# Two-network transformer kernel on one core: three RMS norms applied behind the products that use them

## The reference, cut to what matters

```python
def rms_norm(x, g):
    xf = x.astype(jnp.float32)
    y = xf * lax.rsqrt(jnp.mean(xf * xf, axis=-1, keepdims=True) + NORM_EPS)
    return (y * g.astype(jnp.float32)).astype(x.dtype)

def swiglu(h, w_gate, w_up, w_down):
    return (jax.nn.silu(h @ w_gate) * (h @ w_up)) @ w_down

def odd_mixer(h, positions, w_qkv, w_out):
    q, k, v = jnp.split((h @ w_qkv).reshape(b, s, 3 * DIL_HEADS, HEAD_DIM), 3, axis=2)
    o = dilated_attention(rope(q, positions), rope(k, positions), v)
    return o.reshape(b, s, -1) @ w_out

for layer in range(DEPTH):                      # DEPTH = 2
    x = x + mixers[layer](rms_norm(x, mix_norms[layer]))
    x = x + memory_cross_attention(rms_norm(x, xn), rms_norm(mem, mn), wq, wkv, wo)
    x = x + swiglu(rms_norm(x, fn), wg, wu, wd)
```

## Time and profile before

| | us |
|---|---|
| median of 3 runs | 2158.86 |
| lowest and highest run | 2158.0, 2161.35 |
| the profiled execution, its time | 2164.88 |
| its span in the trace | 2163.1 |
| PE busy | 2038.2 |
| DVE busy | 1088.8 |
| ACT busy | 864.9 |
| POOL busy | 166.6 |

### The profile page before, as it was taken

One profiled execution on the slowest core, in us unless ns is written; L12 is line 12 of the kernel. 1 busy time (PEld: TensorE's weight loads), 2 busy tenths in 40 slices (PEclk: granted clock), 3 DMA queues, 4 the chain that ended last, 5 costly groups with the idle time before them and its releaser, 6 DMA issues.

```text
span 2163.1 us, 34406 instructions
## 1 busy us (share of the span) xinstructions
PE 2038.2 (94%) x14816; PEld 1804.7 (83%) x14816; DVE 1088.8 (50%) x1683; ACT 864.9 (40%) x1227; POOL 166.6 (8%) x165
## 2 busy tenths in 40 slices
PE   7799899899998999999999999999999798999998
PEld 7769899889697999978688877777777687998997
DVE  5555544455555455523534445444444525566554
ACT  4554533343644444523622334222222425444442
POOL 0030100002204000001520000000000003000000
PEclk9899899999998999989999999999999999999999
DMA  7254387764744555512633334445444421664553
GB/s 215 90 187 156 106 199 201 189 173 156 234 156 118 181 189 166 157 55 65 189 108 102 103 98 137 158 154 170 142 149 145 131 74 29 187 192 143 176 178 107
DMA packets 327077, 317.09 MB, mean 147 GB/s; under 512 B 12917, under 2 KB 311676, under 8 KB 326670
## 3 DMA queue, kind: packets, MB, share of 16 engines
q1 hardware_dynamic: 320080, 297.82, 44.7%
q0 software_dynamic: 3904, 12.03, 2.8%
q10 hardware_dynamic: 2942, 5.04, 0.7%
HBM read 306.01 MB, written 8.85 MB: 146 GB/s over the span
## 4 chain that ended last, share of the span: by engine, by line
PE 77%; DVE 9%; DMA 7%; ACT 5%; issue 1%; POOL 0%; ACTq 0%; SPq 0%; DVEq 0%; POOLq 0%
PE acc L631 21%; PE acc L632 20%; PE acc L633 20%; DVE w_low L1713 5%; ACT w_high L1253 3%; DMA raw<-in_l_w_up 2%; PE pss L789 2%; PE pst L800 1%; PE acc L646 1%; PE acc L647 1%; PE acc L648 1%; DMA raw<-in_l_w_down 1%; DMA raw<-in_w_mod 1%; PE acc L718 1%; PE acc L815 1%
## 5 line engine op out<-in xcount | busy, mean ns | idle before, releaser
L1713 DVE TENSOR_TENSOR w_low<-raw,w_high 128x2048 fp32r<-128x2048 f32 (+3 forms) x252 | 539.4, 2140 | 398.2 <-ACT w_high L1253 397.6
L631 PE MATMUL acc<-normed,w_high 128*128 128x256 f32 (+2 forms) x2008 | 641.5, 319 | 21.3 <-DVE w_low L1713 20.2
L632 PE MATMUL acc<-normed,w_high 128*128 128x256 f32 (+2 forms) x2008 | 633.3, 315 | 0.0
L633 PE MATMUL acc<-normed,w_low 128*128 128x256 f32 (+2 forms) x2008 | 632.9, 315 | 0.0
L1253 ACT ACTIVATE w_high<-raw 128x2048 fp32r<-128x2048 f32 (+3 forms) x252 | 447.3, 1775 | 381.0 <-PE acc L633 296.2
L631 PEld LDWEIGHTS acc<-normed,w_high 128*128 128x128 f32 (+1 forms) x2008 | 386.9, 193 | 55.2 <-DVE w_low L1713 27.1
L633 PEld LDWEIGHTS acc<-normed,w_low 128*128 128x128 f32 (+1 forms) x2008 | 386.9, 193 | 22.8
L632 PEld LDWEIGHTS acc<-normed,w_high 128*128 128x128 f32 (+1 forms) x2008 | 387.1, 193 | 22.2
L631 PE MATMUL acc<-inner,w_high 128*128 128x256 f32 (+2 forms) x1232 | 388.4, 315 | 5.2 <-DVE inner L1726 2.4
L632 PE MATMUL acc<-inner,w_high 128*128 128x256 f32 (+2 forms) x1232 | 385.5, 313 | 0.0
L633 PE MATMUL acc<-inner,w_low 128*128 128x256 f32 (+2 forms) x1232 | 385.0, 312 | 0.0
(11 more groups left out here) (214 smaller groups left out, 2131.8 us busy)
## 6 DMA issues: line engine op xcount, KB each, us to landing
raw<-in_w_ff SPq DMA_DIRECT2D x64, 1024.0 KB, 5.5
raw<-in_w_mod SPq DMA_DIRECT2D x48, 1024.0 KB, 5.2
raw<-in_w_in SPq DMA_DIRECT2D x48, 512.0 KB, 3.8
raw<-in_l_w_gate SPq DMA_DIRECT2D x22, 1024.0 KB, 5.6
raw<-in_l_w_up SPq DMA_DIRECT2D x22, 1024.0 KB, 6.1
raw<-in_w_in SPq DMA_DIRECT2D x18, 1024.0 KB, 5.3
raw<-in_l_w_down SPq DMA_DIRECT2D x16, 1024.0 KB, 5.6
raw<-in_l_w_qkv SPq DMA_DIRECT2D x12, 1024.0 KB, 5.2
```

Of the source, the lines that this page charges most:

```text
L631: mm(dst, lh, rh, start=i == 0, stop=False)
L632: mm(dst, lh, rl, start=False, stop=False)
L633: ins = mm(dst, ll, rh, start=False, stop=i == n - 1)
L1713: V.tensor_tensor(WL[:, s % NSPLIT, 0:nw], RAW[:, slot_of[u], 0:nw], WH[:, s % NSPLIT, 0:nw].bitcast(F32), ALU.subtract).then_inc(w_low, 1)
```

## The change

In the three norms, x times the norm's weight (without the row of reciprocal roots) is split and multiplied; the row is applied to the products.

- `gained_highs` (ACT) writes the high part of x times weight straight from x as soon as a residual bank is added, and behind each pair the squares. `gained_low` (DVE) writes the low part. The buffer in between and `highs` are gone for these norms.
- PE begins the next product with tiles that arrive one by one (`one_by_one`), and does `mean_square` behind that first unit and `spread` behind the second.
- `rooted_row` (DVE) copies the spread row to SBUF (RROW, in `scores` 2). `times_row` (DVE) moves a product bank to SBUF and multiplies it with the row.
- FFN: the gate bank goes through `times_row`; ACT's silu reads and writes that SBUF tile; DVE multiplies it with the row again (for the up product) and then with the up bank. On ACT the copy of the next gate unit now stands ahead of silu.
- Mixer of layer 1: q and k go through `times_row` on DVE instead of ACT's copy. For v the row is needed along partitions: `spread(column=True)` makes it with four more matmuls (RCOL), and ACT's copies of v are scaled by it. The rotary products come one unit later behind their product. `memory(1)` moves behind the first `times_row`.

The diff (context cut, eight blanks of indentation left out):

```diff
@@ -179,7 +179,9 @@
 SCRATCH = VEC[:, 117:128]
-ROOTED, EPS2 = VEC[:, 244:252], VEC[:, 252:253]
+ROOTED, EPS2, RCOL = VEC[:, 244:252], VEC[:, 252:253], VEC[:, 253:255]
+RROW = SM[:, 2, 0:S]
+RROW2 = bass.AP(tensor=RROW.tensor, offset=RROW.offset, ap=[list(RROW.ap[0]), [0, 2], [1, S]])
 SKEW = nc.dram_tensor("skew", [2, 120, 64, 127], F32, kind="Internal").ap()
@@ -746,7 +749,7 @@
-    def spread(T, at=0, dst=PST, to=None):
+    def spread(T, at=0, dst=PST, to=None, column=False):
         w, sel = T // 4, const("spread")
@@ -754,6 +757,11 @@
                      start=True, stop=True)
+        if column:
+            for j in range(4):
+                lo = w * (j % 2)
+                ins = mm(dst[lo:lo + w, T + j // 2:T + j // 2 + 1], RSTD[:, at:at + w], sel[:, P * j:P * j + 1],
+                         start=True, stop=True)
         ins.then_inc(spread_done, 1)
@@ -885,6 +893,12 @@
+    def one_by_one():
+        base = st["store"]
+        st["store"] += KD
+        return lambda k: base + k + 1
     def turn_in(src):
@@ -909,10 +923,7 @@
     for l in range(2):
-        if l:
-            mean_square(sq1, KD, S)
-            spread(S)
-        ready = by_tile(S)
+        ready = one_by_one() if l else by_tile(S)
         st["store"] += 4
@@ -966,14 +977,20 @@
         else:
-            for i in range(9):
+            out = []
+            for i in range(10):
+                out.append(st["acc"])
                 if i < 8:
...
                     values(1)
-                if i:
-                    rotate(dil_raw[i - 1:i], const("rot64"), "dil", st["acc"] - 2 - (i > 1))
-            values(2)
+                if i == 0:
+                    mean_square(sq1, KD, S)
+                elif i == 1:
+                    spread(S, column=True)
+                else:
+                    rotate(dil_raw[i - 2:i - 1], const("rot64"), "dil", out[i - 2])
+            values(1)
             attention(dil_tasks, MODS, lead=lambda: values(1), tail=heads_product)
@@ -985,16 +1002,20 @@
         project(2, ot, m=4, kt=4, ready=by_head_tile(4))
-        mean_square(sq1, KD, S)
-        spread(S)
-        ready = by_tile(S)
+        ready = one_by_one()
         done = {}
...
             tiles = FFN_CHUNKS[c][1]
+            if kind == "in" and c == 0:
+                project(1, at_pair, ready=ready)
+                mean_square(sq1, KD, S)
+                project(1, at_pair)
+                spread(S)
+                project(tiles - 2, at_pair)
+            elif kind == "in":
+                project(tiles, at_pair)
             if kind == "in":
-                project(tiles, at_pair, ready=ready)
-                ready = None
                 st["store"] += tiles // 2
@@ -1290,6 +1311,24 @@
+    def gained_highs(units, gain):
+        nc.scalar.activation(SCRATCH[:, st["roots"] % 11:st["roots"] % 11 + 1], EPSC[:], ACT.Sqrt)
+        st["roots"] += 1
+        for u in range(units):
+            if u < units - 1:
+                split()
+            for i in range(4 * u // units, 4 * (u + 1) // units):
+                g = st["acc"] + i
+                act.wait_ge(acc_free[g % 4], g // 4 + 1)
+                for k in (2 * i, 2 * i + 1):
+                    st["store"] += 1
+                    nc.scalar.activation(at_pair.high[:, k, 0:S], XC[:, k, 0:S], ACT.Copy,
+                                         scale=VEC[:, gain + k:gain + k + 1]).then_inc(high_done, 1)
+                for k in (2 * i, 2 * i + 1):
+                    nc.scalar.activation(sq1[:, k, :], XC[:, k, 0:S], ACT.Square).then_inc(sq_done, 1)
+        st["acc"] += 4
     def root(nt, T, at=0, bias=EPSC):
@@ -1414,11 +1453,6 @@
     for l in range(2):
-        if l:
-            root(KD, S)
-            split()
-            highs(norm_chunks(S))
-            highs(mem_chunks())
         if l == 0:
@@ -1476,16 +1510,24 @@
         else:
-            act.wait_ge(skew_w, 16 * 18)
-            for i, dst in enumerate(dil_raw):
-                copy_out(dst, shape2, 64 ** -0.5 if i < 4 else 1.0)
+            g = st["acc"]
+            st["acc"] += 1
+            split()
+            root(KD, S)
+            split()
+            highs(mem_chunks())
+            split(7)
+            st["acc"] += 13
+            act.wait_ge(acc_free[g % 4], g // 4 + 1)
+            def v_lead(i):
+                b, free = bank()
+                for t in range(NB):
+                    ins = nc.scalar.activation(v_dil[:, t, S * i:S * i + S], b[:, S * t:S * t + S], ACT.Copy,
+                                               scale=RCOL[:, t:t + 1])
+                ins.then_inc(free, 1)
                 split()
-                st["acc"] += i > 0
-
-            def v_lead(i):
-                copy_out(v_dil[:, :, S * i:S * i + S], shape2)
-                split()
-                st["acc"] += i == 0
+                st["acc"] += i < 2
@@ -1515,27 +1557,30 @@
         attention(x_tasks, lead=lambda: vx_lead(1))
-        residual_squares(2, sq1, S)
-        root(KD, S)
+        gained_highs(2, vcol[f"l{l}_ffn_norm"])
         split()
-        highs(norm_chunks(S))
         for kind, c in ffn_turns:
...
                 for m in range(0, tiles, 2):
-                    b, free = bank()
-                    i, g = st["sig"], st["acc"]
-                    if m or c:
-                        act.wait_ge(stored, st["store"])
-                    nc.scalar.activation(SM[:, i % 2, :], b[:], ACT.Silu).then_inc(free, 1)
+                    i, g = st["sig"] % 2, st["acc"]
+                    st["acc"] += 1
+                    if m == c == 0:
+                        root(KD, S)
+                    split()
+                    act.wait_ge(acc_free[g % 4], g // 4 + 1)
+                    nc.scalar.activation(SM[:, i, :], SM[:, i, :], ACT.Silu).then_inc(gated, 1)
                     st["sig"] += 1
-                    split()
+                    g = st["acc"]
                     st["acc"] += 1
...
                 act.wait_ge(gain_done, 3)
-                residual_squares(4, sq1, S, gain=ROOTED if l else None)
+                if l:
+                    residual_squares(4, sq1, S, gain=ROOTED)
+                else:
+                    gained_highs(4, vcol["l1_mix_norm"])
             elif l and (kind, c) == ffn_turns[-2]:
@@ -1816,6 +1861,28 @@
+    def gained_low(m, gain):
+        for k in m:
+            st["store"] += 1
+            dve.wait_ge(high_done, st["store"])
+            V.scalar_tensor_tensor(at_pair.low[:, k, 0:S], XC[:, k, 0:S], VEC[:, gain + k:gain + k + 1],
+                                   at_pair.high[:, k, 0:S].bitcast(F32), ALU.mult, ALU.subtract)\
+                .then_inc(stored, 1)
+    def rooted_row(column=False):
+        spreaded()
+        if column:
+            link(V.tensor_copy(RCOL, PST[:, S:S + 2]))
+        link(V.tensor_copy(RROW, PST[:, 0:S]))
+    def times_row(dst, g, scale=1.0):
+        dve.wait_ge(acc_full, g + 1)
+        V.scalar_tensor_tensor(dst, PSACC[g % 4][:].rearrange("p (a n) -> p a n", a=2), scale, RROW2, ALU.mult,
+                               ALU.mult).then_inc(acc_free[g % 4], 1)
     def memory(l, lo=0, hi=4):
@@ -1996,11 +2063,8 @@
     for l in range(2):
-        norm(XC, norm_chunks(S), S, vcol[f"l{l}_mix_norm"], lead=None if l else split)
-        if l:
-            split()
-            memory(1)
         if l == 0:
+            norm(XC, norm_chunks(S), S, vcol["l0_mix_norm"], lead=split)
             split()
@@ -2028,14 +2092,24 @@
         else:
-            for i in range(9):
+            g = st["acc"]
+            st["acc"] += 1
+            split()
+            inverted(S)
+            split()
+            rooted_row(column=True)
+            dve.wait_ge(skew_w, 16 * 18)
+            times_row(dil_raw[0], g, 64 ** -0.5)
+            memory(1)
+            for i in range(1, 10):
+                if i < 8:
+                    times_row(dil_raw[i], st["acc"], 64 ** -0.5 if i < 4 else 1.0)
                 st["acc"] += 1
                 split()
-                if i:
-                    rope(dil_raw[i - 1:i], sin64)
-            split()
+                if i > 1:
+                    rope(dil_raw[i - 2:i - 1], sin64)
             attention(dil_tasks, MODS)
-            st["acc"] += 3
+            st["acc"] += 2
         for m in banks(8, S):
@@ -2045,12 +2119,14 @@
         st["acc"] += 3 + 2
-        for i in range(2):
-            for m in banks(8, S)[2 * i:2 * i + 2]:
-                residual_bank(m, None, S)
-            if i == 0:
+        gain = vcol[f"l{l}_ffn_norm"]
+        for m in banks(8, S):
+            residual_bank(m, None, S)
+            if m[0]:
+                gained_low([m[0] - 2, m[0] - 1], gain)
+            if m[0] == 2:
                 split()
-        norm(XC, norm_chunks(S), S, vcol[f"l{l}_ffn_norm"])
+        gained_low([KD - 2, KD - 1], gain)
         split()
@@ -2058,13 +2134,23 @@
                     st["acc"] += 1
-                    split()
```

(22 more changed lines are left out.)

1 line of the change is left out of this document (added).

## The result

The changed kernel takes 2168.13 us (median of 7 runs, 2165.6 to 2176.25), the kernel before beside it 2158.0 (7 runs, 2154.17 to 2161.35): 1.0057 times, 95% interval 1.0038 to 1.0077. The forecast was 2160.9, a plus of 2.0, with a range up to 2167.5. The four series of this kernel that there are by now give +12.3, +5.9, +7.7 and +4.6 us on the mean of their runs (standard errors 1.9, 1.5, 1.2, 1.5). Weighted by these that is +7.2.

What follows compares the result with a forecast made beforehand. TensorE, busy 94% of the span, was taken as the bound, so only its idle or slow stretches count. Terms -2.3 - 1.3 + 0.2 + 5.4 = +2.0 us on the median 2158.86 gave 2160.9, range 2158 to 2165 (8 in 10: 2152.5 to 2167.5).

Steps and rivals of the forecast that it cites:

- Layer 0's FFN norm: Layer 0's FFN: gate 0 without a gap, waits before up 0 and up 1; 2.3 us gained (1.0 to 3.1).
- it costs nothing, because up 2 waits for its DMA longer still: Layer 0's FFN: a low clock after the 2.5 us wait before up 1 costs 0, hidden by up 2's DMA wait.
- no term depends on what lies between: Whole kernel: the +2.0 us worked out on the profiled execution also holds for the median, 6.0 us lower.
- Layer 1's mixer norm: Layer 1's qkv units: 1.3 us gained (0 to 2.5) despite a 4.3 us wait before unit 3; v's half copies lose 0.2.
- the case for which the forecast had a gain of 0.6 only: Layer 1's mixer norm: the first 2.0 us of waiting also bring the clock down, leaving a gain of 0.6 us.
- Layer 1's FFN norm: Layer 1's FFN: GpSimd's bias addition holds VectorE's low parts to its end; 5.4 us lost (4.1 to 7).
- The second fall of the clock: Layer 1's FFN, behind the 2.5 us wait before up 1: low clock again, 1.5 us, half of it taken.
- The order that I called decided by 0.1 us: Layer 1's FFN norm: whether POOL's addition starts before gate 0's split; if so, 6.1 us lost instead of 4.8.
- The first rival: Layer 1's FFN norm: low parts not held by GpSimd, only the split; total -3.0, 2155.9 us, chance 0.15.
- nothing lands on the path: Steady FFN pairs: VectorE gets 1.4 us more a pair, yet the deciding step from up's end to the next split is unchanged.
- The slow rival: Layer 0's FFN pairs: silu waits behind a late gate's copy, up to 0.9 us a time, 4 to 5 us; 2165.5, chance 0.25.
- The sign that the prediction named for this rival: Layer 0's FFN: PE waits clearly longer than before for split weights, behind pairs whose gate landed late.

Runs made afterwards that it cites:

- the quiet pair: The kernel before and the changed kernel, each without 14 of GpSimd's 16 layout DMAs in layer 0's FFN: 2149.47 and 2152.44 us.
- mixer_only: Only layer 1's mixer norm changed, against the kernel before: 2153.62 us, ratio 0.9983.
- l0_ffn_only: Only layer 0's FFN norm changed, against the kernel before: 2158.04 us, ratio 0.9994.
- l1_ffn_only: Only layer 1's FFN norm changed, against the kernel before: 2163.82 us, ratio 1.002.
- whole_pieces: All three norms changed and GpSimd's bias addition cut into 16 instructions, against the kernel before: 2153.49 us, ratio 0.9994.
- l0_mixer_pieces: Layer 0's FFN norm and layer 1's mixer norm changed, bias addition in 16 pieces, against the kernel before: 2166.7 us, ratio 1.0012.
- mixer_pieces: Only layer 1's mixer norm changed, bias addition in 16 pieces, against the kernel before: 2153.36 us, ratio 0.9977.
- silu_first: All three norms changed, silu and VectorE's gate product ahead of the next gate's copy and split, against the kernel before: 2167.22 us, on another chip 2158.77.
- silu_pieces: All three norms changed, silu ahead of the next gate's copy, bias addition in 16 pieces, against the kernel before: 2162.88 us, then 2149.89.
- quiet_whole: All three norms changed, 14 of GpSimd's 16 layout DMAs in layer 0's FFN left out, against the kernel before: 2152.44 us, ratio 0.9982.

## Why the prediction was wrong

The forecast was +2.0; measured were +10.1 by the medians of the first series and +7.2 (1.4) over all four. Two terms were put at nothing that are not nothing: the place of silu in the steady pairs (4.1 us) and, in layer 0, the clock behind the new wait before up 1 (1.6 us).

- **Layer 0's FFN norm, forecast -2.3.** Gate 0 without a gap, 0.75 us of wait before up 0 (0.9 forecast), up 1 at +22.7 (+22.7) behind a wait of 2.35 (2.5): right. Wrong is "it costs nothing, because up 2 waits for its DMA longer still". The clock takes 1.6 us in the quiet pair. The wait that was to hide it, 1.96 us before up 2, stands in the trace of before and in none of the other 19. So it was wrong, too, that "no term depends on what lies between" the traced execution and the median. The norm is worth about 2.8 - 1.6 = 1.2. (In the sum for gate unit 0, 242.66 + 0.81 + 0.87 + 2.29 is 246.6 and not 246.2, unless the first low part starts behind the first high part, as it does in after; nothing hung on it.)
- **Layer 1's mixer norm, forecast -1.3 and +0.2.** The wait before unit 3 is 3.56 (4.3 forecast); unit 3 takes 8.3 us (7.3) in after and 7.5 in mixer_only. From the last down product to the first scores it is 82.2 us on the mean of the fifteen traces with this change and 84.3 on that of the five without: -2.1 (0.7), inside the range of the term. In after and two others of the fifteen qkv unit 0 also ran at the low clock (7.5 us for 6.0), the case for which the forecast had a gain of 0.6 only.
- **Layer 1's FFN norm, forecast +5.4 (4.1 to 7).** The mechanism is as written: a low part held for 8.76 us, ending with POOL's addition, TensorE idle for 7.31, up 0's split done at 692.90, which is 15.5 us after the last product before the norm (15.9 forecast). Up 1 stands at +31.5 on the mean of the ten traces, with the old norm at +27.3 (27.1 to 27.7 in four): 4.2 lost. The second fall of the clock, for which I had taken half of 1.5 us, came in three of the ten and adds 0.45, so the term is +4.7, in the range and 0.7 less than taken. Gate 0's remaining matmuls took 5.9 us instead of 6.7. The order that I called decided by 0.1 us came out both ways.
 The Trainium skill (SBUF — State Buffer, section Who interferes with whom) says that any VectorE instruction with two SBUF inputs contends with a GpSimd instruction that reads SBUF, and that whoever issues first keeps the shared port pair. The trace agrees, for scalar_tensor_tensor too (8.76 us for 0.88). The first rival, low parts not held, is thereby out.
- **The steady pairs, "nothing lands on the path".** This step failed. It was worked out for a pair whose loads are in time, and for that it holds: layer 1's FFN, beside which no layout DMAs run, takes 177.0 us from up 1 to its last down product, and before 177.0. Layer 0's is another matter. The slow rival, silu behind a late gate, had a chance of 0.25 and 4 to 5 us; putting silu ahead again gave 4.1 (1.1). It was no rival to the sum but a term of it. The rows of before had its condition in them: six gates landed late, for 11.2 us in all. With silu behind them ScalarE waits 15.6 to 23.7 us for gates in the same FFN, in part because it now comes to that copy earlier. The sign that the prediction named for this rival, a clearly longer wait of PE for split weights in layer 0's FFN, does not show in the trace of after (10.8 us for 13.5).

The terms as now measured, added up for each kernel, against the timed means (silu's term is itself taken from differences between timed kernels, the others from traces):
```
terms: l0 norm -1.2, mixer -2.1, l1 norm +4.7 (in pieces -1.5; old norm in pieces -1.3), silu's place +4.1 (quiet +2.0)
kernel                 sum    timed mean (standard error)
all three norms       +5.5    +7.2 (1.4), four series
l0_ffn_only           +2.9    -0.2 (1.6)
mixer_only            -2.1    -3.4 (1.5)
l1_ffn_only           +4.7    +5.3 (2.0)
whole_pieces          -0.7    -2.9 (1.3)
l0_mixer_pieces       -0.5    +1.4 (1.3)
mixer_pieces          -3.4    -5.0 (1.5)
silu_first            +1.4    +3.4 (1.4), +0.8 (1.5)
silu_pieces           -4.8    -3.4 (2.2), -7.8 (1.8)
quiet_whole - before  +3.4    +3.5 (1.0)
```
All lie within two standard errors. The four series of the kernel after scatter from +4.6 to +12.3, and why the first stands apart is open. Layer 0's norm alone should have shown silu's cost (+2.9) and did not (-0.2). The other pair that differs in this norm alone, l0_mixer_pieces and mixer_pieces, gives +6.4 (2.0), on two chips; the two together give +2.4 (1.3). That silu's place costs, is measured, and so is that it costs nothing where the loads are in time. That late gates are the way by which it costs is what is left, and the rows of a late pair suggest it; the stretches of layer 0's FFN don't show it.

The range reached to 2167.5, 0.6 short of the median. Rival and forecast were kept as alternatives, each with the other's term at nothing; added, they would have given +6.5, or 2165.4.

## What to carry to other kernels

Before VectorE gets new work that reads two SBUF tensors, look in the trace for long GpSimd instructions in that place: a long one held each such instruction here to its end, and cut into 16 it took turns with them. When a step moves behind a copy or a split that may wait for a load, count how often that load is late in the trace of before and charge the wait to the step; a rival whose cause already stands in the rows belongs into the sum. And a wait of 2 us on TensorE is not free because the next load is late as well: look what clock stands behind it, and whether the late load is there in more than one trace.

## What the runs showed of the hardware

- One GpSimd instruction of 9.67 us held two VectorE instructions of 0.44 us for 8.76 us; 16 short ones slowed the same pair to 1.83, and took 18.27 us in all, where the one took 9.67.
- The same wait of 2.35 us on TensorE, before the same weight unit, was followed by a clock of 0.70 to 0.73 over 5.75 us in all 14 traces in layer 0, and in layer 1 by 0.70 in six traces and 1.00 in seven. It cost 1.5 us where the clock fell.
- The granted clock falls at other places from run to run in untouched code. The stretch 80 to 100 us, in before and then in after, both the same program:
```profile
80.00:100.00 20.00, 16.45 (x118) 14.79 (x110) 10.60 (x17) 6.16 (x11) 4.05 (x3) 0.85 0.00 1
```
```profile
80.00:100.00 20.00, 17.25 (x122) 15.52 (x123) 10.09 (x16) 4.42 (x12) 4.05 (x3) 0.70 0.03 12
```
 At 0.85 the clock is at the lower of its two levels (1.2 GHz) for a third of the time, at 0.70 for over half, with TensorE not filled in either, and the first products of the next stage come at 101.8 or 105.1 us. That is 3 us of scatter which belong to no change.
